# Differential attention's rotary embedding: half-head rows exchanged by DMA in blocks of 16 instead of by a matrix product

## The reference

```python
def _rope(x, pos):
    d = x.shape[-1]
    half = d // 2
    inv = ROPE_THETA ** (-jnp.arange(half, dtype=jnp.float32) / half)
    ang = pos.astype(jnp.float32)[:, None] * inv[None, :]
    cos, sin = jnp.cos(ang), jnp.sin(ang)
    xf = x.astype(jnp.float32)
    x1, x2 = xf[..., :half], xf[..., half:]
    return jnp.concatenate([x1 * cos - x2 * sin, x2 * cos + x1 * sin], axis=-1).astype(x.dtype)

def _diff_attention(q, k, v, lam, sub_g, lam_init):
    B_, S_, _ = q.shape
    pos = jnp.arange(S_)
    q = _rope(q.reshape(B_, S_, DA_HEADS, 2, DA_QK_DIM).transpose(0, 2, 3, 1, 4), pos)
    k = _rope(k.reshape(B_, S_, DA_HEADS, 2, DA_QK_DIM).transpose(0, 2, 3, 1, 4), pos)
    ...
        s = jnp.einsum('bhmqd,bhmkd->bhmqk', qi, k).astype(jnp.float32) * scale
```

## Time and profile before

| | us |
|---|---|
| median of 3 runs | 2738.35 |
| lowest and highest run | 2738.26, 2739.26 |
| the profiled execution | 2739.44 |
| its span, first to last instruction | 2738.1 |
| PE busy | 2695.2 |
| DVE busy | 1645.8 |
| ACT busy | 1027.5 |

### The profile page before, as it was taken

One profiled execution on the slowest core, in us unless ns is written; L12 is line 12 of the kernel. 1 busy time (PEld: TensorE's weight loads), 2 busy tenths in 40 slices (PEclk: granted clock), 3 DMA queues, 4 the chain that ended last, 5 costly groups with the idle time before them and its releaser, 6 DMA issues.

```text
span 2738.1 us, 35258 instructions
## 1 busy us (share of the span) xinstructions
PE 2695.2 (98%) x14505; PEld 2211.3 (81%) x14505; DVE 1645.8 (60%) x3335; ACT 1027.5 (38%) x1753; POOL 14.8 (1%) x43
## 2 busy tenths in 40 slices
PE   8999999999999999999999999999999999999999
PEld 5788888889888888766888889888888666888888
DVE  6766555357767455778776746753345778633334
ACT  4642332435222244555422224223234555422223
POOL 1000000000000000000000000000000000000000
PEclk9999999999999999999999999999999999999999
DMA  8255333133666333401555524642232511232331
GB/s 252 82 178 168 114 93 116 62 108 124 200 190 196 102 115 88 125 32 32 185 185 184 189 93 134 204 134 92 92 108 85 147 47 32 63 107 93 100 97 66
DMA packets 343305, 329.38 MB, mean 120 GB/s; under 512 B 10338, under 2 KB 333670, under 8 KB 343144
## 3 DMA queue, kind: packets, MB, share of 16 engines
q1 hardware_dynamic: 343060, 327.11, 38.4%
q10 hardware_dynamic: 84, 0.02, 0.0%
HBM read 320.81 MB, written 2.10 MB: 118 GB/s over the span
## 4 chain that ended last, share of the span: by engine, by line
PE 93%; DVE 4%; SPq 1%; ACT 1%; DMA 1%; issue 0%; DVEq 0%
PE bank L540 26%; PE bank L542 25%; PE bank L541 25%; PE bank L582 3%; PE bank L568 2%; PE bank L570 2%; PE bank L569 2%; PE bank L2354 2%; PE bank L2383 1%; PE bank L1377 1%; PE bank L1367 1%; PE bank L2041 1%; DVE w_lo L508 1%; DVE E L2480 0%; DMA raw<-in_nsa_cmp_w 0%; DMA mw<-in_w_mod 0%
## 5 line engine op out<-in xcount | busy, mean ns | idle before, releaser
L540 PE MATMUL bank<-h_lo,w_hi 128*128 128x512 f32 (+1 forms) x2448 | 925.5, 378 | 3.6 <-DVE h_lo L707 2.2
L542 PE MATMUL bank<-h_hi,w_lo 128*128 128x512 f32 (+1 forms) x2448 | 901.6, 368 | 0.0
L541 PE MATMUL bank<-h_hi,w_hi 128*128 128x512 f32 (+1 forms) x2448 | 899.6, 367 | 0.0
L508 DVE TENSOR_TENSOR w_lo<-raw,w_hi 128x1024 fp32r<-128x1024 f32 (+1 forms) x422 | 490.9, 1200 | 299.1 <-ACT w_hi L502 298.9
L502 ACT ACTIVATE w_hi<-raw 128x1024 fp32r<-128x1024 f32 (+1 forms) x422 | 421.4, 1034 | 343.0 <-PE bank L542 326.9
L540 PEld LDWEIGHTS bank<-h_lo,w_hi 128*128 128x128 f32 x2448 | 461.8, 189 | 87.7 <-issue 8.5
L541 PEld LDWEIGHTS bank<-h_hi,w_hi 128*128 128x128 f32 x2448 | 462.2, 189 | 77.1 <-issue 5.2
L542 PEld LDWEIGHTS bank<-h_hi,w_lo 128*128 128x128 f32 x2448 | 460.9, 188 | 77.4
L540 PE MATMUL bank<-a_lo,w_hi 128*128 128x512 f32 (+1 forms) x1056 | 391.4, 371 | 0.0
L542 PE MATMUL bank<-a_hi,w_lo 128*128 128x512 f32 (+1 forms) x1056 | 384.9, 365 | 0.0
L541 PE MATMUL bank<-a_hi,w_hi 128*128 128x512 f32 (+1 forms) x1056 | 384.5, 364 | 0.0
(11 more groups left out here) (309 smaller groups left out, 2566.3 us busy)
## 6 DMA issues: line engine op xcount, KB each, us to landing
swf<-in_w_ada SPq DMA_DIRECT2D x60, 1024.0 KB, 7.9
raw<-in_ffn_w_gate SPq DMA_DIRECT2D x44, 1024.0 KB, 5.4
raw<-in_ffn_w_up SPq DMA_DIRECT2D x44, 1024.0 KB, 5.4
raw<-in_w_in SPq DMA_DIRECT2D x40, 1024.0 KB, 5.2
raw<-in_ffn_w_down SPq DMA_DIRECT2D x32, 1024.0 KB, 5.2
raw<-in_w_in SPq DMA_DIRECT2D x34, 512.0 KB, 5.2
raw<-in_ffn_w_down SPq DMA_DIRECT2D x16, 768.0 KB, 4.5
mw<-in_w_mod SPq DMA_DIRECT2D x8, 1024.0 KB, 11.7
```

What stands on the lines that cost most here:

```text
L508: nc.vector.tensor_tensor(o, r, half(w_his[place_of[i]], i, h)[0].bitcast(F32), ALU.subtract).then_inc(*w_lo.up((i, h)))
L540: nc.tensor.matmul(o, w1, al, start=start, stop=False)
L541: nc.tensor.matmul(o, w1, ah, start=False, stop=False)
L542: return nc.tensor.matmul(o, w2, ah, start=False, stop=stop)
```

## The change

The four pieces p = 0 to 3 take the way of the others. R32 is no longer in the constants. `pe_rope` is gone with its four products a layer. `sp_rope` exchanges blocks of 16 rows for p below 4, so it issues eight DMAs of 16 rows and 2 KB a row for each piece. The table of sines carries the sign of the exchanged half. In SP's list the swaps of pieces 0 and 1 stand after the loads of step dk, those of 2 and 3 after the loads of step xa. In DVE's list both w_lo steps ahead of rotation 0 and 1 are now made before rotation 0.

```diff
@@ host_constants
-    c["R32"], c["R64"] = rot(32), rot(64)
+    c["R64"] = rot(64)
...
-            "k_da": np.concatenate(table(32, np.arange(S)), 1)}
+            "k_da": np.concatenate([cd, sd], 1).astype(np.float32)}
@@ sp_rope, pe_rope
     def sp_rope(l, p):
+        n = 16 if p < 4 else 32
         sp.wait_ge(act, ("rq", l, p))
-        for i in range(4):
-            nc.sync.dma_start(swaps[p % 2][i * 32:i * 32 + 32, :], pair(p)[0][(i ^ 1) * 32:(i ^ 1) * 32 + 32, :]).then_inc(
-                *swap_in[p % 2].up((l, p), 16))
-
-    def pe_rope(l, p):
-        t = bank(("rr", l, p), M_ROPE)
-        pe.wait_ge(act, ("rq", l, p))
-        nc.tensor.matmul(t[:, :], cst["R32"], pair(p)[0][:, :], start=True, stop=True).then_inc(
-            *pe.up(("rr", l, p)))
+        for r in range(0, 128, n):
+            o = r ^ n
+            nc.sync.dma_start(swaps[p % 2][r:r + n, :], pair(p)[0][o:o + n, :]).then_inc(*swap_in[p % 2].up((l, p), 16))
@@ dve_rope
-        if p < 4:
-            dve.wait_ge(pe, ("rr", l, p))
-            dve.wait_ge(dve, PREV)
-            nc.vector.tensor_tensor(q0[:, :], ps.of(("rr", l, p))[:, :], sin, ALU.mult).then_inc(
-                *dve.up(("rs", l, p), lets=("rr", l, p)))
-        else:
-            q0 = swaps[p % 2]
-            dve.wait_ge(swap_in[p % 2], (l, p))
-            nc.vector.tensor_tensor(q0[:, :], q0[:, :], sin, ALU.mult).then_inc(*dve.up(("rs", l, p)))
+        q0 = swaps[p % 2]
+        dve.wait_ge(swap_in[p % 2], (l, p))
+        nc.vector.tensor_tensor(q0[:, :], q0[:, :], sin, ALU.mult).then_inc(*dve.up(("rs", l, p)))
@@ pe_mixer
-            pe_rope(l, m)
...
-            pe_rope(l, 2 + m)
@@ dve_mixer
-        dve_w(("dk", l))
+        dve_w(("xa", l))
         dve_rope(l, 0)
-        dve_w(("xa", l))
         dve_rope(l, 1)
@@ sp_mixer
-        swap_after = {("nq", l, 0): (4, 5), ("nq", l, 1): (6, 7), ("kk", l): (8, 9)}
+        swap_after = {("dk", l): (0, 1), ("xa", l): (2, 3), ("nq", l, 0): (4, 5), ("nq", l, 1): (6, 7), ("kk", l): (8, 9)}
```

More of the change, by code:

```diff
@@ L75, in host_constants @@
     l2 = np.concatenate([co, si, *table(64, end)], 1)
+    cd, sd = table(32, np.arange(S))
+    sd = np.where((p % 32 < 16)[:, None], -sd, sd)
     return {"k_res": res.astype(np.float32), "k_l1": l1.astype(np.float32), "k_l2": l2.astype(np.float32),
-            "k_da": np.concatenate(table(32, np.arange(S)), 1)}
-RES = ["ident", "ones", "bones", "tril", "C", "R32", "R64", "ca", "any", "quad"]
+            "k_da": np.concatenate([cd, sd], 1).astype(np.float32)}
+RES = ["ident", "ones", "bones", "tril", "C", "R64", "ca", "any", "quad"]
 RESW = {"C": 512, "any": 4, "quad": 4}
```

## The result

| | before | after |
|---|---|---|
| median of 9 runs each, on the same chip | 2738.43 us (2737.95 to 2740.08) | 2731.85 us (2730.16 to 2733.26) |
| ratio to before, with its 95% interval | 1 | 0.9975 (0.9966 to 0.9984) |
| the profiled execution: time, span | 2739.44, 2738.1 us | 2731.40, 2730.1 us |
| granted clock of TensorE, mean | 0.996 | 0.996 |

The kernel is 6.6 us faster. The forecast was 2731.5 us.

The account below looks back on a forecast made before the run. PE was taken to bound the kernel: eight products at 0.86 us take 6.9 us off the profiled 2739.44 us, nothing added, giving 2732.6; the median lies 1.1 lower, so 2731.5 us. Range 2730.2 to 2735.0 us.

Parts of the forecast that it names:

- What bounds the kernel: Whole kernel: PE, busy 98% of the span; a change is worth what it takes off PE's line of work.
- the price of a product: Rope products on PE, start of each layer's mixer: 0.86 us each, 3.44 us a layer, 6.88 us in all.
- DVE: Rotations 0 to 3: multiply duration unchanged, earlier w_lo of dv free, rope 3 done 1.6 us before PE wants it.
- SP: SP's queue: 64 more DMAs, 0.62 us per issue, 2.0 us to landing; piece 3's swap 2.6 us early for DVE.
- "single outliers": Swap issues on SP: single outliers of 0.9 and 1.3 us fit into 2.6 + 1.6 = 4.2 us of slack.
- The first (slack used up): Swap chain to rope 3: 1 to 3 us late at PE in both layers, 2733.5 to 2737.5 us; chance 0.13.
- The second (SP's issue rate): SP's queue: PE waits from a pitch of 0.86 us, slower above 0.97; 2769 us at 1.47; chance 0.06.
- its formula: Last swap lands at about 1033.8 + 31 p + 0.4 + 2.0, p the issue pitch; PE waits if later than 1062.9.
- The third (copies one after the other): Swaps on the DMA engines: copies serialize at 2.0 us each, 40 us late, 2812 us; chance 0.01.
- The fourth (another wait in the products' place): PE at dv or nq0: a covered wait for w_lo or a bank replaces the products, 2738.4 us; chance 0.04.
- The two loads that moved: SP's loads of nq0 and w1, now behind swaps: land at 1049.1 and 1062.7, before their readers need them.
- The smaller load of k_res: Second table load at the start, 64 KB smaller: 0.3 us of transfer once, counted as nothing.

Follow-up runs that it names:

- Experiment 2: Changed kernel with eight products of the same shape put back on PE, result unused, DVE waiting for them, swaps kept: 2738.70 us, 1.0001 of before.
- experiment 4: Kernel before with its eight rope products kept but on one-pass fp32r operands, dropping the low part: 2732.91 us, 0.9981 of before.
- experiment 1: Kernel before without its eight rope products and no swaps, DVE multiplying the unexchanged copy by the sines: 2730.92 us, 0.9975 of before.
- experiment 7: Changed kernel with 8-row swaps, twice the issues, for some pieces only: pieces 2 and 3, 2751.36 us; piece 3 alone, 2736.79 us.
- Experiment 6: Changed kernel with every swap of pieces 0 to 3 cut into two of 8 rows, same bytes, 64 more issues: 2769.97 us, 1.0117 of before.
- experiment 8: Changed kernel with 8-row swaps for pieces 0 to 3, half issued by GpSimd's queue, half by SP's: 2731.73 us, 0.9977 of before.
- Experiment 9: Changed kernel with the four bones products of the head norm on one-pass operands, dropping the low part: 2728.74 us, 0.9965 of before.
- experiment 5: Changed kernel with the load of nq0 issued ahead of the swaps of pieces 0 and 1: 2731.15 us, 0.9975 of before.

## Why the prediction was right

**What bounds the kernel, and the price of a product.** Right. PE's line of work got shorter and nothing came late. 0.86 us a product, read in the chain and again from starts in the timeline, gave 3.44 us a layer; 3.47 was measured in each. Experiment 2 put the 0.86 back, experiment 4 left 0.24 of it.

**DVE.** Right. The first sine multiply no longer waits, w_lo waits for ACT's split in its place, and rope 3's add ends at 1062.95 us where the text had 1062.7. PE starts its scores at 1064.54 against 1064.3; the start of the stretch itself is 0.27 us later in this execution. The 1.6 us of slack at DVE is there. The layers stand 1038.19 us apart (copy of piece 0 to copy of piece 0) against 1042.02 before, 3.8 us less where the text had 3.4; experiment 1, with the same 31.17 us from copy to scores, has 1039.21, so what is beyond 3.47 is a difference between executions.

**SP.** Right in the median, too low in the mean; the slack covered the error. The pitch of 0.62 us was read from four swaps that happened to have no long issue among them; over 16 it is 0.65 to 0.72 us. So swap 1 was in at 1046.85 and not at 1045.1. The last issue of piece 3 began at 1057.5 and not at 1056.6. With the usual 2.0 us it landed at 1059.5, and DVE wanted it at 1061.55: 2.0 us early, where the text had 2.6. The slack at SP and at DVE together is 3.6 us, not 4.2. That "single outliers" fit into it was right.

**The rivals.** The first (slack used up) did not happen: 31.17 us in both layers, as with no swap at all. Piece 3 cut in two (experiment 7) shows how near it is: 8 more issues of 0.69 us are 5.5 us, which used up the 3.6 us of slack and made PE wait for the 1.9 us left (1.6 us in layer 1). The second (SP's issue rate) has the right mechanism and the right form. Experiment 6 is that rival made real: the issue costs the same whatever the rows, so cutting copies doubles the time. But its price was too low. By its formula, with two issues of 0.69 us for each pitch, the last swap lands at 1033.8 + 31 x 1.38 + 2.4 = 1079.0, which is 16.1 us late, less 3.44, twice: 2763.7 us. It was 2770.0. The lateness itself came out as the formula has it: 17.2 and 15.9 us. What it left out is the clock that falls during the wait, 3.4 and 3.2 us behind the scores. The third (copies one after the other) is refuted by the landings, 2.0 us each for copies issued 0.7 us apart, and by experiment 8, where two queues start them twice as often and they land in 1.9 us. The rule on disjoint partition halves that the text cited from the Trainium skill, "DMA: Bandwidth & Descriptors", section "Rules for kernel authors", cost nothing here. It isn't refuted either: where nothing but 8-row swaps run back to back, the DMA engines are busy for a share of 0.14 (window 1068 to 1076 of experiment 6), so how the bytes of two copies share the engines could hardly show in these times. The fourth (another wait in the products' place) is refuted by the profile after, in which PE waits for nothing in this stretch. Experiment 9 shows that it was a rival worth naming: for another product such a wait does take part of the gain.

**Left at zero.** The two loads that moved cost nothing: that of nq0 by experiment 5, and that of w1 since its first use stands 12.39 us behind the scores in both kernels. The smaller load of k_res is not visible: the start of the stretch is later by 0.27 us, not earlier by 0.3, and it lies anywhere from 1032.70 to 1033.66 us over the traces of these kernels.

## What to carry to other kernels

Where the chain of waits is one engine's own work, the piece of an instruction in that chain is the most that its removal gives back, and all of it if no other wait takes its place; what replaces it has only to fit into slack, so follow each replacement on its own queue up to the instant at which its reader wants it. For many small copies, count issues by their mean over a long row, outliers included, and not the bytes: cutting a copy in two costs a whole issue, and a second queue buys back what one queue can't issue in time. When lateness does reach TensorE, price it above the wait, since the clock may fall too.

## What the runs showed of the hardware

- An issue from SP of a copy from one SBUF tile to another takes the same 0.59 to 0.62 us for 32, 16 and 8 rows of 512 floats, 0.65 to 0.72 us apart on average over 16 or 32 in a row, with single ones up to 1.8 us. GpSimd's queue issued the same 8-row copies in 0.52 us.
- TensorE's granted clock fell to 0.50, the 1.2 GHz level, during or after idle times of 13.9, 12.8, 7.6, 7.1, 2.5 and 1.9 us, and stayed full after two of 1.6 us. After one of 2.76 us at the same place of the program it fell in one layer and stayed full in the other, in the kernel after and in the kernel before. A fall cost 1.6 us beyond the wait after the 1.9 us, 2.0 and 2.3 us from the scores on after the 7.6 and 7.1 us, and 3.4 and 3.2 us after the 12.8 and 13.9 us. These cases make no rule.
- A float32 product of 128 x 128 by 128 x 512 takes two records of 0.43 us in the chain, and one of the one-pass type 0.24 us.
